# Index scores of 64 rows issued in pairs in the last mixer of a fused two-block kernel

## The reference

```python
# q_idx (B,T,8,64), k_idx (B,T,64), w_idx (B,T,8); blocks of 128 query rows
iscore = relu(einsum('bqhd,bsd->bqhs', qib, k_idx))    # 8 heads, 64 numbers each
iscore = einsum('bqh,bqhs->bqs', wb, iscore)           # weighted sum over heads
iscore = where(admiss, iscore, NEG)
_, sel = top_k(iscore, 128)
```

## Time and profile before

| | us |
|---|---|
| median of 3 runs | 2215.6 (2213.72 to 2216.07) |
| profiled execution, its own time | 2219.75 |
| span of the profiled execution | 2218.3 |
| TensorE matmul busy in it | 2085.8 (94%) |
| TensorE weight loads busy | 1700.6 (77%) |
| VectorE busy | 1162.8 (52%) |
| ScalarE busy | 867.0 (39%) |
| selection stage, from the first feature product to the last | about 1792.8 to 1931 of the span |

### The profile page before, as it was taken

The page is one execution under the profiler, slowest core; times in us unless marked ns, Lnnn a source line. Parts: engine busy times, 40 slices in busy tenths (PEclk is TensorE's granted clock), DMA queues, the critical chain, the costliest instruction groups (busy, mean ns, idle before and its releaser), DMA issues.

```text
span 2218.3 us, 24613 instructions
## 1 busy us (share of the span) xinstructions
PE 2085.8 (94%) x9984; PEld 1700.6 (77%) x9984; DVE 1162.8 (52%) x2252; ACT 867.0 (39%) x1553; POOL 242.5 (11%) x185
## 2 busy tenths in 40 slices
PE   6999999999997999999999998999999799999797
PEld 6987788887876777788887888877777566877575
DVE  5425553332236565453333226998974428766553
ACT  5435542222232455442222213467552223366520
POOL 1001110000011000010000003677700000000000
PEclk9999999999998998999999999999999899999998
DMA  6320122223323211222332232322223212211211
GB/s 231 103 96 31 67 86 95 95 95 105 114 78 112 76 55 71 95 86 96 98 103 102 83 107 95 98 77 92 77 85 109 81 57 76 76 39 39 76 57 57
DMA packets 28800, 192.60 MB, mean 87 GB/s; under 512 B 3264, under 2 KB 3408, under 8 KB 7440
## 3 DMA queue, kind: packets, MB, share of 16 engines
q1 hardware_dynamic: 24848, 175.96, 23.3%
q0 software_dynamic: 3264, 12.99, 1.7%
q10 hardware_dynamic: 576, 2.10, 0.2%
HBM read 186.84 MB, written 4.19 MB: 86 GB/s over the span
## 4 chain that ended last, share of the span: by engine, by line
PE 80%; DVE 13%; ACT 5%; issue 1%; DMA 0%; POOL 0%; SPq 0%; DVEq 0%; ACTq 0%; POOLq 0%
PE bank L398 23%; PE bank L400 22%; PE bank L399 22%; DVE bank L2121 5%; PE bank L1807 2%; DVE WL L370 2%; PE bank L1698 1%; PE bank L1795 1%; ACT WH L356 1%; PE bank L1708 1%; PE bank L2262 1%; PE bank L1273 1%; PE bank L1184 1%; PE bank L543 1%; PE bank L1800 1%
## 5 line engine op out<-in xcount | busy, mean ns | idle before, releaser
L398 PE MATMUL bank<-XH,WH 128*128 128x512 f32 (+1 forms) x1504 | 596.3, 397 | 15.7 <-DVE XL L559 10.3
L400 PE MATMUL bank<-XH,WL 128*128 128x512 f32 (+1 forms) x1504 | 566.9, 377 | 0.0
L399 PE MATMUL bank<-XL,WH 128*128 128x512 f32 (+1 forms) x1504 | 566.4, 377 | 0.0
L370 DVE TENSOR_TENSOR WL<-RAW,WH 128x2048 fp32r<-128x2048 f32 x128 | 293.2, 2292 | 453.0 <-ACT WH L356 452.9
L356 ACT ACTIVATE WH<-RAW 128x2048 fp32r<-128x2048 f32 x148 | 282.3, 1908 | 329.2 <-PE bank L400 323.5
L398 PEld LDWEIGHTS bank<-XH,WH 128*128 128x128 f32 x1504 | 285.6, 190 | 85.4 <-issue 25.6
L399 PEld LDWEIGHTS bank<-XL,WH 128*128 128x128 f32 x1504 | 285.9, 190 | 55.0 <-issue 6.6
L400 PEld LDWEIGHTS bank<-XH,WL 128*128 128x128 f32 x1504 | 285.1, 190 | 53.1 <-issue 0.6
L2121 DVE SCALAR_TENSOR_TENSOR bank<-conv_in,cols,bank 128x512 f32<-128x512 f32 x290 | 198.3, 753 | 1.1
L398 PE MATMUL bank<-WH,XH 128*128 128x428 f32 (+2 forms) x416 | 159.5, 383 | 11.4 <-DVE XL L559 6.3
L399 PE MATMUL bank<-WL,XH 128*128 128x428 f32 (+2 forms) x416 | 154.6, 372 | 0.0
(11 more groups left out here) (333 smaller groups left out, 2990.2 us busy)
## 6 DMA issues: line engine op xcount, KB each, us to landing
RAW<-weights SPq DMA_DIRECT2D x164, 1024.0 KB, 4.8
row_a<-rows POOLq DMA_DIRECT2D x7, 512.0 KB, 5.9
row_b<-rows POOLq DMA_DIRECT2D x6, 512.0 KB, 6.1
x_res<-x SPq DMA_DIRECT2D x1, 2048.0 KB, 16.7
kv<-mem_park POOLq DMA_DIRECT2D x2, 1024.0 KB, 5.1
out<-x_res ACTq DMA_DIRECT2D x4, 512.0 KB, 2.6
mem_tok<-mem SPq DMA_DIRECT2D x1, 1024.0 KB, 4.9
mem_tok<-mem POOLq DMA_DIRECT2D x1, 1024.0 KB, 8.3
```

Source lines behind the costliest of these rows:

```text
L370: dve.tensor_tensor(WL[j][:, :], RAW[j][:, :], WH[j][:, :].bitcast(F32), ALU.subtract).then_inc(*lo.mark())
L398: pe.matmul(ps, ah, bh, start=first, stop=False)
L399: pe.matmul(ps, ah, bl, start=False, stop=False)
L400: return pe.matmul(ps, al, bh, start=False, stop=last)
```

## The change

The step of an even head issues its own score and right behind it that of the odd head after it. The step of an odd head issues nothing on TensorE. ScalarE's and VectorE's parts stay where they were. Nothing else of the kernel changes, and the number of instructions is the same.

```diff
     def index_step_pe(k, t):
-        if k < IH:
-            w, r = (t + 1) * P, slice(IHD * (k % 2), IHD * (k % 2) + IHD)
-            ps = take_bank("spare", "index", t, k)
-            pe.matmul(ps[:, 0:w], qiT[r, k // 2, t * P:(t + 1) * P], kiT[r, 0:w], start=True, stop=True).then_inc(
-                *T.mark("full", "index", t, k))
+
+        if k < IH and k % 2 == 0:
+            w = (t + 1) * P
+            for k in (k, k + 1):
+                r = slice(IHD * (k % 2), IHD * (k % 2) + IHD)
+                ps = take_bank("spare", "index", t, k)
+                pe.matmul(ps[:, 0:w], qiT[r, k // 2, t * P:(t + 1) * P], kiT[r, 0:w], start=True, stop=True).then_inc(
+                    *T.mark("full", "index", t, k))
```

## The result

The changed kernel takes 2199.59 us (2198.93 to 2201.43, 4 runs) against 2215.29 before on the same chip: a ratio of 0.9932, interval 0.9916 to 0.9947, so 15.7 us less. I had forecast 7.9 us less, 2207.7, and a range down to 2205.0.

What follows compares the result with a forecast made beforehand. TensorE, without a gap in the selection stage, was taken as the bound. Switches 4.6 plus overlap 3.9 us, less 0 or 1.2 for loads, gave 8.5 or 7.3; the middle, 7.9, meant 2207.7 us, range 2205.0 to 2213.0.

Steps and rivals of the forecast that it cites:

- What bounds the kernel: Selection stage: TensorE has no gap, so a microsecond less of TensorE is a microsecond less of the stage.
- (1): Score visits: 24 trips into the half-array mode become 12, each saving 0.38 us; 4.6 us.
- (2): Inside a pair: odd head's first pass runs beside even head's second, one pass less per pair; 3.9 us.
- Rival A: Inside a pair: no overlap, odd head's passes wait for the even head's; 4.6 us, 2211.0; chance 0.22.
- rival E: Inside a pair: both passes lie under the other head's; 12.3 us, 2203.3; chance 0.02.
- (3): Odd head's first load: may wait for the even head's second pass; 0 or 1.2 us of the overlap lost.
- (4): Odd heads' scores, moved four to five feature steps earlier: operands and bank are ready, smallest cover 8.6 us; cost nothing.
- (5): DMA queues: TensorE issues no DMA and nothing is moved past the queues; no cost.
- (6): Stage's start, 7.1 us at 0.50 clock: the low stretch ends at the same moment; no term.
- Rival D: Clock behind pairs falls to 1.2 GHz, 3.3 us per low stretch; slower, 2220.9 with three; chance 0.04.
- Passing the gain on: Tile 3's scores: VectorE would come 0.9 us late to a lowering, then catch up in the next tile's idle time.
- rival C: Last tile: `sel` comes after TensorE, so the gain is absorbed; 2213 to 2215.6; chance 0.04.

Runs made afterwards that it cites:

- e1_same_rows: The change, but with the odd heads' scores computed from the even heads' rows, 0 to 63; 2210.16 us, ratio 0.9981.
- e2_full_rows: The kernel before, scores unpaired, but each taken over all 128 rows; 2204.13 us, ratio 0.9958.
- e7_order_0213: The change with four heads in a row instead of two, in the order 0, 2, 1, 3 (4, 6, 5, 7); 2198.03 us, single run.

## Why the prediction was wrong, point by point

**What bounds the kernel** held. TensorE was without a gap in the stage before and after, and all that was taken from it came through to the end.

**(1) The switches**, 12 x 0.38 = 4.6 us: right in sum. The comparison of a 64-row with a 128-row product gave the mechanism and the size; `e1_same_rows` (4.1 us by the medians) and `e2_full_rows` (1.10 for 1.50 us a visit) measure the same by the edit of one operand. The prediction's two places for the 0.38, though, make only 0.09 + 0.10. The rest lies between them: from the score's start to the L398 behind it there are 0.84 us (1840.22 to 1841.06) where two passes take 0.64.

**(2) The overlap** is the term that was mis-sized: forecast one pass a pair, 3.9 us; it was both, 7.7. The sentence that failed is "MATMULs start in order, so the odd head's first pass can run beside the even head's second". I took it that the odd head's first pass may not start ahead of the even head's second. The rows never showed that; they show only single products, with whole-array passes on both sides. In the profile after, the first passes of both heads start together (x2 over 0.59 us), and `e7_order_0213` shows that not even a second product waiting for one half holds up the other half. Rival A's distances (1.71, 2.14 and 2.57) are those of `e1_same_rows`, where both heads share a half, and not those of the change. The last bound in (2) had it, "If even both passes lay under the other head's, it would be 7.7", and rival E carried it with its total, 12.3; I gave it 0.02. With an unmeasured operation and a known mechanism for concurrency, the full bound deserved far more than that. The Trainium skill, TensorE: Matmul & The Clock Gate, Part 3, has products in different row groups side by side, at about 4 ns more for each further one. By that rule alone the second head is free, and the sum beside it is 12.3 and not the 8.5 of the prediction. Here the visit with two heads is at most 0.01 us longer than with one. The same part of the Trainium skill calls MATMULs strictly first in, first out, in start and in end; across the halves `e7_order_0213` doesn't agree, with 2.15 us where that order gives 2.77, and the measurement decides.

**(3) The odd head's load**, 0 to 1.2 us lost: nothing was lost. Four loads cover 0.30 us, where two covered 0.29 in the earlier trace rows.

**(4) Banks and order, (5) the queues**: right. From the stage's first product on, TensorE waited for nothing up to the first sparse attention product; no relu and no bank held it up.

**(6) The low clock**, put at no term: it gave 1.7 us. I had reasoned that the low stretch would end at the same moment. It ended 3.3 us earlier in the profile after, and as early in the other four that restart at the same distance with a visit to both halves. Rival D looked for the clock's effect with the wrong sign: behind no pair did the clock fall (1.00 from 1792.8 to 1915.9).

**Passing the gain on**: right. With more taken from TensorE than forecast, VectorE did come late, as said. Its lowerings in order of time, as in the earlier trace rows:

```profile
1858.69 2.28 DVE L370 TENSOR_TENSOR WL<-RAW,WH 128x2048 fp32r<-128x2048 f32 x1
...
1873.90 2.29 DVE L370 TENSOR_TENSOR WL<-RAW,WH 128x2048 fp32r<-128x2048 f32 x1
1882.57 2.29 DVE L370 TENSOR_TENSOR WL<-RAW,WH 128x2048 fp32r<-128x2048 f32 x1 [0.44 <-ACT WH L356]
1893.45 2.29 DVE L370 TENSOR_TENSOR WL<-RAW,WH 128x2048 fp32r<-128x2048 f32 x1 [2.65 <-ACT WH L356]
1904.33 2.29 DVE L370 TENSOR_TENSOR WL<-RAW,WH 128x2048 fp32r<-128x2048 f32 x1 [1.13 <-ACT WH L356]
```

Before, the third of these had 2.64 us of idle time ahead of it:

```profile
1900.90 2.29 DVE L370 TENSOR_TENSOR WL<-RAW,WH 128x2048 fp32r<-128x2048 f32 x1 [2.64 <-ACT WH L356]
```

The idle time ahead of the lowerings in tile 3's scores is gone (2.00 and 0.73 before), it shrinks from 2.64 to 0.44 at the next, and from then on it is what it was: 2.65 for 2.64 and 1.13 for 1.12. VectorE had caught up a unit before `sel` of the last tile was due, and rival C stayed away.

**The sum**: 4.6 + 7.7 + 1.7 = 14.0 us, and 0.5 more between the visits; the stage gives 14.4, the medians 15.7 in one comparison (interval 11.7 to 18.6) and 12.6 in the other (10.8 to 16.4). The overlap in full, 12.3 us or 2203.3, leaves the forecast's range by itself; the clock's 1.7 on top of my 7.9, 2206.0, would not have. So it is the overlap of (2) that failed, and the clock came on top.

## What to carry to other kernels

Look for 64-row products among 128-row ones: each visit to the half array costs a fixed 0.38 us here, for 256 to 512 columns alike, and a second product in the other half, right behind the first and into another bank, costs at most 0.01 us. So gather as many of them into one visit as banks allow; of the two orders tried here neither was better. And where a bound says "fully hidden" and no row speaks against it, give that end a real chance instead of the middle.

## What the hardware showed that I had not expected

Two float32 products of 64 rows each, issued one behind the other, take the time of one: 1.50 and 1.71 us a visit for two heads as for one. A product that waits for one half doesn't hold up the one behind it for the other half (2.15 us for four heads of 384 columns in either order). A 64-row product in a 128-row stream costs 0.40 us more than the same product over 128 rows. And the clock rose 4.0 us behind a restart when the first 64-row visit used both halves (five profiles), 7.3 to 7.4 when it used one (four profiles), all nine restarting 2.8 to 2.9 us after it had fallen.
